# First mixer of a two-layer diffusion backbone: the sum of the squared attention outputs as two fp32r products instead of one fp32 product

## The reference, cut to what matters

```python
def _rms(x, w):
    x32 = x.astype(jnp.float32)
    y = x32 * lax.rsqrt(jnp.mean(x32 * x32, axis=-1, keepdims=True) + EPS)
    return (y * w.astype(jnp.float32)).astype(x.dtype)

def _attn_post(o, subln_w, lam_init):
    B, L = o.shape[:2]
    return (_rms(o, subln_w) * (1.0 - lam_init)).reshape(B, L, ATTN_WIDTH)
```

## Time and profile before

| | us |
|---|---|
| median of 3 runs (1651.87 to 1652.13) | 1652.09 |
| the profiled execution | 1654.46 |
| its span, from the first to the last instruction | 1652.8 |
| TensorE busy in the span | 1640.0 (99%) |
| VectorE busy | 1081.4 (65%) |
| ScalarE busy | 623.1 (38%) |
| GpSimd busy | 84.9 (5%) |
| mean granted TensorE clock | 0.999 of full |

### The profile page before, as it was taken

How to read it: one execution, slowest core, us unless ns; L and a number is a source line. 1 busy time by engine, 2 the same in 40 slices (tenths; PEclk the granted TensorE clock), 3 DMA queues, 4 the chain that set the end, 5 groups by cost and what they waited for, 6 DMA issues and landing times.

```text
span 1652.8 us, 22863 instructions
## 1 busy us (share of the span) xinstructions
PE 1640.0 (99%) x9030; PEld 1404.9 (85%) x9030; DVE 1081.4 (65%) x1686; ACT 623.1 (38%) x955; POOL 84.9 (5%) x150
## 2 busy tenths in 40 slices
PE   8999999999999999999999999999999999999999
PEld 4888888889778898888888998888888997899999
DVE  5677777546778667777763367777523577776654
ACT  5423222124655452232222252323222365565542
POOL 0001001000000100110100000101000000100000
PEclk9999999999999999999999999999999999999999
DMA  9555555532211234555553235555433232355554
GB/s 375 175 198 194 188 203 184 186 102 81 86 64 52 77 103 168 202 189 194 198 185 101 77 104 202 185 197 193 139 102 95 97 103 77 115 177 182 178 184 148
DMA packets 69606, 250.37 MB, mean 151 GB/s; under 512 B 7552, under 2 KB 8576, under 8 KB 69376
## 3 DMA queue, kind: packets, MB, share of 16 engines
q1 hardware_dynamic: 51072, 181.84, 33.6%
q0 software_dynamic: 18432, 67.12, 10.6%
HBM read 247.88 MB, written 1.05 MB: 151 GB/s over the span
## 4 chain that ended last, share of the span: by engine, by line
PE 95%; DVE 2%; ACT 1%; DMA 1%; issue 1%; POOLq 0%; SPq 0%; POOL 0%; DVEq 0%; ACTq 0%
PE ps L1343 30%; PE ps L1345 30%; PE ps L1344 30%; PE ps L1687 1%; PE ps L1599 1%; PE ps L1655 1%; DVE wlo L812 1%; PE ps L1669 0%; DMA h<-x_t 0%; DVE nmax L1171 0%; PE ps L1448 0%; PE ps L1527 0%; ACT whi L451 0%; PE ps L1529 0%; DVE cx L1072 0%
## 5 line engine op out<-in xcount | busy, mean ns | idle before, releaser
L812 DVE TENSOR_TENSOR wlo<-raw,whi 128x1024 fp32r<-128x1024 f32 x320 | 392.4, 1226 | 441.7 <-ACT whi L451 441.3
L1343 PE MATMUL ps<-xh,whi 128*128 128x512 f32 (+1 forms) x1580 | 582.4, 369 | 2.3 <-POOL xl L430 1.7
L1344 PE MATMUL ps<-xl,whi 128*128 128x512 f32 (+1 forms) x1580 | 568.7, 360 | 0.0
L1345 PE MATMUL ps<-xh,wlo 128*128 128x512 f32 (+1 forms) x1580 | 568.7, 360 | 0.0
L451 ACT ACTIVATE whi<-raw 128x1024 fp32r<-128x1024 f32 x320 | 338.2, 1057 | 584.9 <-PE ps L1345 507.3
L1343 PEld LDWEIGHTS ps<-xh,whi 128*128 128x128 f32 x1580 | 298.8, 189 | 55.3 <-issue 6.1
L1344 PEld LDWEIGHTS ps<-xl,whi 128*128 128x128 f32 x1580 | 299.0, 189 | 47.4 <-issue 3.8
L1345 PEld LDWEIGHTS ps<-xh,wlo 128*128 128x128 f32 x1580 | 298.8, 189 | 45.1
L1343 PE MATMUL ps<-ah,whi 128*128 128x512 f32 (+2 forms) x976 | 323.1, 331 | 0.4 <-DVE shared_b L1032 0.4
L1345 PE MATMUL ps<-ah,wlo 128*128 128x512 f32 (+2 forms) x976 | 322.2, 330 | 0.0
L1344 PE MATMUL ps<-al,whi 128*128 128x512 f32 (+1 forms) x800 | 272.2, 340 | 0.0
(11 more groups left out here) (144 smaller groups left out, 1135.1 us busy)
## 6 DMA issues: line engine op xcount, KB each, us to landing
raw<-wstream SPq DMA_DIRECT2D x320, 512.0 KB, 3.4
wm<-wmod POOLq DMA_DIRECT2D x128, 512.0 KB, 4.6
wm<-wmod SPq DMA_DIRECT2D x8, 1024.0 KB, 17.1
h<-x_t SPq DMA_DIRECT2D x4, 512.0 KB, 7.1
cb<-cols SPq DMA_DIRECT2D x1, 1024.0 KB, 20.5
out_t<-h SPq DMA_DIRECT2D x8, 128.0 KB, 2.3
K<-cols SPq DMA_DIRECT2D x1, 907.0 KB, 19.4
K<-cols SPq DMA_DIRECT2D x1, 265.5 KB, 2.9
```

Of the source, the lines that this page charges most:

```text
L812: dve.tensor_tensor(wlo[:, n % RING, :, :].rearrange("p a b -> p (a b)"), raw[:, n % RING, :], whi[:, n % SPL, :, :].rearrange("p a b -> p ...
L1343: pe.matmul(out_ap, hi_w, hi_x, start=start, stop=False)
L1344: pe.matmul(out_ap, hi_w, lo_x, start=False, stop=False)
L1345: return pe.matmul(out_ap, lo_w, hi_x, start=False, stop=stop)
```

## The change

In the first mixer `tile_square` writes the squares twice: in float32 into `lnk` and rounded to fp32r into the first half of `osq`, which lies over `sqk`. VectorE subtracts one from the other into the second half of `osq` (`tile_square_low`, in step e + 3, behind `split_next` and `unit_dif`, and behind the `tile_scale` of an earlier tile where there is one). TensorE adds up both halves with a matrix of ones in fp32r, which ScalarE copies once, in the first feed-forward stage. The second mixer keeps the fp32 product.

```diff
+        osq = out_squares.enter_context(nc.sbuf_tensor("osq", [P, 2, T], F32R))
+        ones_r = sb("ones_r", [P, P], F32R)
...
                     if f == 0 and j == 1:
                         act.wait_ge(cb_in, 16)
                         act.activation(cb[:, :, :], cb[:, :, :], ACT.Silu).then_inc(cb_done, 1)
+                        act.activation(ones_r[:, :], col("ones", 0, P), ACT.Copy).then_inc(ones_in, 1)
...
                 def tile_square(t):
                     g = TB[l] + t
                     act.wait_ge(of_done, g + 1)
+                    if l == 0:
+                        heads = of[:, t, :, :].rearrange("p h q -> p (h q)")
+                        act.wait_ge(rq_done, 8)
+                        if t >= 1:
+                            act.wait_ge(orstd, g)
+                        act.activation(lnk[:, :], heads, ACT.Square).then_inc(osq_done, 1)
+                        act.activation(osq[:, 0, :], heads, ACT.Square).then_inc(osq_hi, 1)
+                        return
...
+                def tile_square_low(t):
+                    dve.wait_ge(osq_hi, t + 1)
+                    dve.tensor_tensor(osq[:, 1, :], lnk[:, :], osq[:, 0, :].bitcast(F32), ALU.subtract)\
+                        .then_inc(osq_lo, 1)
...
                     for t, e in enumerate(ENDS[l]):
+                        if l == 0 and p == e + 3:
+                            tile_square_low(t)
                         if p == e + 5:
                             tile_scale(t)
...
                     pe.wait_ge(osq_done, g + 1)
 
                     pe.wait_ge(evac, EV[l] + CQ + p // 2)
+                    if l == 0:
+                        pe.wait_ge(osq_lo, t + 1)
+                        pe.matmul(ps[:, idle_bank(p), :], ones_r[:, :], osq[:, 0, :], start=True, stop=False)
+                        pe.matmul(ps[:, idle_bank(p), :], ones_r[:, :], osq[:, 1, :], start=False, stop=True)\
+                            .then_inc(ostat, 1)
+                        return
                     pe.matmul(ps[:, idle_bank(p), :], col("ones", 0, P), sqk[:, g % 2, :], start=True, stop=True)\
                         .then_inc(ostat, 1)
```

More of the change, by code:

```diff
@@ L176, in program @@
         cx = sb("cx", [P, 8, T])
+        out_squares = ExitStack()
+        osq = out_squares.enter_context(nc.sbuf_tensor("osq", [P, 2, T], F32R))
+        out_squares.close()
         sqk = sb("sqk", [P, 2, T])
@@ L253, in program @@
         of_done = sem("of_done")
+        ones_in = sem("ones_in")
         osq_done = sem("osq_done")
+        osq_hi = sem("osq_hi")
+        osq_lo = sem("osq_lo")
         ostat = sem("ostat")
```

## The result

The changed kernel takes 1659.83 us in the median of 5 runs (1659.49 to 1662.46), the kernel before 1652.09 us (5 runs, 1651.44 to 1652.29). The ratio is 1.0049, with a 95% interval of 1.0038 to 1.006: slower by 7.7 us. The forecast was 1659.5. The profiled execution took 1661.43 us, with a span of 1659.8 us.

A forecast was written before the change was run, and what follows sets the result against it. TensorE was taken to end the chain for 95% of the span. Tile delays 0.0 + 1.4 + 0.4 + 4.5, end gap -0.4 and clock +1.5 gave +7.4 us, so 1659.5 for the median; range 1655.5 to 1662.0.

The forecast's parts named there:

- The product: TensorE, each tile of the first mixer: one 0.86 us product becomes two of 0.23, 0.40 us less, 1.6 in all.
- The place of the low half: VectorE's subtraction stands behind other work and TensorE waits for it; gaps of about 0 to 0.2, 1.7, 0.8 and 4.8 us.
- The steps of the sum: Delays of TensorE in the first mixer: tiles 0.0, +1.4, +0.4, +4.5; end gap -0.4; clock +1.5 us.
- 0.05 + 0.10: TensorE after VectorE's subtraction: 0.05 us to start, plus 0.10 for a weight load that can no longer run ahead.
- GpSimd holds VectorE up twice at tile 3: GpSimd's subtractions go ahead of tile_scale and the low half, lengthening both to about 1.79 us; tile 3 adds 4.5 us.
- Rival (2): GpSimd not ahead twice at tile 3: +3.7 to +4.8 us at full clock, +5.2 to +6.3 with the fall; chance 0.20.
- The clock: TensorE's clock falls to half after the 4.8 us stall at tile 3, costing 1.5 us, bounds 0 and 3.4.
- Rival (1): First mixer: same waits but the clock stays full, +5.9 us, 1658.0; chance 0.18.
- rival (4): The clock falls more than once, after tile 1's gap too, or longer after tile 3: +8.9 to +10.4 us; chance 0.10.
- The gap at the end goes: TensorE's old 0.43 us gap before the products for output rows 0 to 3 is covered: -0.4 us.
- The second square: ScalarE's extra square moves the weight copy, and VectorE's split behind it, by 0.52 us at each tile.
- Rival (3): The wait for the low half is hidden, only the shorter products count: -2.0 us, 1650.1; chance 0.10.

The follow-up runs named there:

- the fastest version: Changed kernel with the low half ahead of the weight split, the last split behind tile_low of tile 1, the first convolution sum behind tile_out of tile 2: 1649.42 us.
- its control: Kernel before, fp32 product and one square, with only the last split and the first convolution sum moved later in VectorE's list: 1651.61 us.
- the high half twice: Changed kernel without the subtraction: TensorE adds the high half two times and waits only for ScalarE's second square: 1652.49 us.
- The low half first: Changed kernel with the low half's subtraction moved ahead of the same step's weight split in VectorE's list: 1652.22 us.

## Why the prediction was right, and where it was not

- *The product, 0.40 us per tile.* Right: 1.6 us between the fastest version and its control, 1.5 between the changed kernel and the fp32 product behind the same wait.
- *The place of the low half sets TensorE's gaps.* Shown. The gaps of 0.23, 1.66, 0.79 and 4.64 us vanish when the subtraction moves ahead of the split, and without it (the high half twice) nothing better comes out. Directly behind the split only the gap of tile 3 is left. The steps of the sum were off by 0.1 us each. A part of that is the pair of products: it starts 0.15 us behind the end of the subtraction at every tile (548.02 behind 546.13 + 1.74), as the prediction's 0.05 + 0.10 has it, but its two starts are 0.31 us apart and not 0.23, so TensorE is free 0.69 us behind the subtraction instead of 0.61.
- *GpSimd holds VectorE up twice at tile 3.* Shown by moving GpSimd: 1.75 and 1.74 us become 0.74 and 0.68, and the gap shrinks from 4.64 to 2.57. Rival (2) fell: both trace and run have GpSimd ahead twice. The Trainium skill (SBUF — State Buffer, Who interferes with whom) lets issue order decide who blocks; GpSimd's record starts at 544.13, tile_scale's at 544.45, and the trace agrees.
- *The clock.* Shown by keeping TensorE busy: 1.6 us, for 1.5 forecast. Rival (1) fell. That the size came so near is in part luck. In the changed kernel the half clock begins 0.5 us behind the restart (548.02), so nearly all of it fell on products; behind the same gap of 4.64 us with the fp32 product it began 1.4 us before the restart and lasted twice as long. That run's trace is also the case of rival (4), two falls in the first mixer; the changed kernel's trace has its second fall only in the second mixer.
- *The gap at the end goes.* Right, -0.4.
- *The second square.* The prediction gave its 0.52 us to the line that leads to the low half, which is right, and nothing to what waits besides. In the changed kernel no gap contradicts that, but TensorE was late there anyway; as a general statement it is wrong, and so was the expectation of the run with the second square alone, which had it hidden at the first three tiles. In the kernel before it costs 1.2 us in the stretch: 0.44 at step 12, where TensorE waits for tile_out of tile 2, and 0.7 at the end. That GpSimd, now ahead of tile_scale, lengthens the gap at the end fits the trace, but no run takes it apart from the later split.
- *Rival (3), the wait hidden.* I priced it at -2.0 us. The low half first is that case, and it gave +0.1 (stretch +0.3). The price left out the two gaps of 0.77 and 1.24 us, and counted the old one at the end as closed. It takes two more moves in VectorE's list to get to -2.1.
- *Forecast of the time.* 7.4 us against 7.7 measured; the terms lie within 0.1 us each.
- *Slips that change nothing.* If VectorE's queue were served first at tile 3, the sum is +3.7 with a full clock, the lower end of rival (2); the prediction calls it the third rival's. The ends of its range, 1655.5 and 1662.0, lie 0.3 us outside what it names them by: 1652.1 + 3.7 = 1655.8 and, for the middle of rival (4), 1661.7.

The cause of the slowdown is thus settled. The copy of the ones was not tried by itself; the pair of kernels with all moves leaves nothing for it.

## What to carry to other kernels

When one engine must now wait for a second one, look first at what stands ahead of the new instruction in the second engine's list, and sum it up from the trace: here four subtractions of 0.7 us, in a place behind a weight split and then a unit of attention or a tile_scale, cost 7.7 us, and in front of these 0.1. A saving on the engine that sets the end arrives only as far as the next instruction that it waits for; read the lists for waits of length zero, which are where the next gap opens. And a gap on TensorE costs more than itself when the clock falls behind it.

## What the runs showed of the hardware

- Half clock followed gaps of 4.64 and 2.98 us, not one of 2.57 (with GpSimd later) nor one of 0.98 behind the filling products; in the second mixer all 13 traces have a gap of 1.50 to 1.52 us with shorter ones ahead of it, and 6 of them half clock behind it. So the length of one gap does not tell. Each fall lasted 3.4 us; the one behind 4.64 us cost 1.6, and in one profiled execution there were two in a row.
- Whether VectorE or GpSimd goes first turned on 0.5 us: GpSimd's record at 542.63 behind the start of tile_scale (542.44) left it at 0.75 us, one at 542.42 ahead of it (542.74) made it 1.79.
